# A 32-tile MLP at the end of a two-net kernel: 24 of its hidden tiles in pairs by Strassen's method, output rows between the products

## What is computed

```python
    u = rms_norm_2(h, norm_mlp_g[l])
    h = h + jnp.square(jax.nn.relu(u @ w_mlp1[l])) @ w_mlp2[l]
return rms_norm_2(h, final_norm_g)
```

## Time and profile before

| | |
|---|---|
| median of 3 runs | 2532.96 us (2532.82 to 2533.18) |
| the profiled execution | 2532.82 us |
| its span | 2531.0 us |
| TensorE (PE) busy | 2511.3 us, 99% |
| DVE busy | 1882.5 us, 74% |
| ACT busy | 1170.4 us, 46% |
| DMA queues, HBM | 97 GB/s over the span |

### The profile page before, as it was taken

The page is one execution under the profiler, slowest core; times in us unless marked ns, Lnnn a source line. Parts: engine busy times, 40 slices in busy tenths (PEclk is TensorE's granted clock), DMA queues, the critical chain, the costliest instruction groups (busy, mean ns, idle before and its releaser), DMA issues.

```text
span 2531.0 us, 35169 instructions
## 1 busy us (share of the span) xinstructions
PE 2511.3 (99%) x13914; PEld 2187.0 (86%) x13914; DVE 1882.5 (74%) x2579; ACT 1170.4 (46%) x1843; POOL 302.8 (12%) x250
## 2 busy tenths in 40 slices
PE   8999999999999999999999999999999999999999
PEld 7899988888999889999888899997888888788887
DVE  8878867777888687887786778876999786642433
ACT  5444445444444444444553444445587445432332
POOL 4000001320000000000024000000286231100001
PEclk9999999999999999999999999999999999999999
DMA  5333333233333323333423233334322423233332
GB/s 155 98 97 102 94 103 92 77 101 90 92 100 109 115 84 97 98 106 103 109 59 100 85 106 94 105 107 128 80 74 74 130 88 113 80 106 100 92 100 83
DMA packets 489962, 248.32 MB, mean 98 GB/s; under 512 B 41922, under 2 KB 486599, under 8 KB 489543
## 3 DMA queue, kind: packets, MB, share of 16 engines
q1 hardware_dynamic: 489346, 245.76, 33.5%
q10 hardware_dynamic: 452, 0.32, 0.1%
HBM read 241.84 MB, written 4.19 MB: 97 GB/s over the span
## 4 chain that ended last, share of the span: by engine, by line
PE 92%; DVE 5%; ACT 2%; issue 1%; DMA 0%; POOL 0%; DVEq 0%; ACTq 0%
PE bank L725 7%; PE bank L727 7%; PE bank L726 7%; PE bank L806 7%; PE bank L805 7%; PE bank L804 7%; PE psS L826 5%; PE psS L827 5%; PE psS L828 5%; PE psT L725 4%; PE psT L727 4%; PE psT L726 4%; PE psT L870 2%; PE psT L872 2%; PE psT L871 2%; PE psS L725 1%
## 5 line engine op out<-in xcount | busy, mean ns | idle before, releaser
L2004 DVE TENSOR_TENSOR wlo<-raw,whi 128x1024 fp32r<-128x1024 f32 (+1 forms) x274 | 362.8, 1326 | 116.7 <-ACT whi L1421 113.5
L725 PE MATMUL bank<-xhi,whi 128*128 128x512 f32 x888 | 349.4, 393 | 1.4 <-issue 1.4
L726 PE MATMUL bank<-xlo,whi 128*128 128x512 f32 x888 | 345.9, 390 | 0.0
L727 PE MATMUL bank<-xhi,wlo 128*128 128x512 f32 x888 | 345.8, 389 | 0.0
L1421 ACT ACTIVATE whi<-raw 128x1024 fp32r<-128x1024 f32 (+1 forms) x271 | 277.1, 1025 | 121.8 <-PE psT L727 92.4
L804 PE MATMUL bank<-xsh,whi 128*128 128x256 f32 x768 | 217.5, 283 | 0.9 <-ACT part L1534 0.7
L805 PE MATMUL bank<-xsl,whi 128*128 128x256 f32 x768 | 217.3, 283 | 0.0
L806 PE MATMUL bank<-xsh,wlo 128*128 128x256 f32 x768 | 217.3, 283 | 0.0
L2067 DVE TENSOR_TENSOR wlo<-tw,whi 128x1024 fp32r<-128x1024 f32 x128 | 156.9, 1226 | 63.1 <-ACT whi L1453 63.0
L826 PE MATMUL psS<-hhi,whi 128*128 128x512 f32 x512 | 200.8, 392 | 0.0
L827 PE MATMUL psS<-hlo,whi 128*128 128x512 f32 x512 | 200.8, 392 | 0.0
(11 more groups left out here) (586 smaller groups left out, 6444.4 us busy)
## 6 DMA issues: line engine op xcount, KB each, us to landing
raw<-in_ffn_wg SPq DMA_DIRECT2D x88, 512.0 KB
raw<-in_ffn_wu SPq DMA_DIRECT2D x88, 512.0 KB
raw<-in_w_mlp SPq DMA_DIRECT2D x64, 512.0 KB
raw<-in_w_in SPq DMA_DIRECT2D x53, 512.0 KB
raw<-in_ffn_wd SPq DMA_DIRECT2D x48, 256.0 KB
raw<-in_ffn_wd SPq DMA_DIRECT2D x32, 384.0 KB
raw<-in_ffn_wd SPq DMA_DIRECT2D x48, 192.0 KB
raw<-in_ffn_wd SPq DMA_DIRECT2D x48, 128.0 KB
```

The costliest lines, as they stand in the source:

```text
L725: pe.matmul(dest, a, rhs_hi(k), start=start and k == 0, stop=False)
L726: pe.matmul(dest, a, rhs_lo(k), start=False, stop=False)
L727: mm = pe.matmul(dest, b_, rhs_hi(k), start=False, stop=stop and k == tiles - 1)
L2004: dve.tensor_tensor(wlo[:, a:a + n], raw[:, a:a + n], whi[:, a:a + n].bitcast(F32), ALU.subtract).then_inc(s_split, 1)
```

## The change

The MLP is written like the windows. Tiles 0 to 7 are made as before (`MPLAIN`). Tiles 8 to 31 are made in 12 windows, two tiles each (`mlp_window`). The two passes are gone: the hidden tiles are in groups of 6, 6, 6, 6 and 8. The output rows of the first four groups (4 x 8 chunks x 6 tiles = 192 tiles of work) are cut in 25 units of 7 or 8, one ahead of the windows and two in each window, and each finished chunk of a group is added to x by DVE (`ffn_group_added`, `k_xa`). The last group's 8 chunks of 8 tiles follow the windows. The quarter sums of x are made beside tiles 2, 3, 4 and 5, each of which takes one unit of TensorE. Hidden tiles go into 14 places: 12 of `hhi`/`hlo` and two laid over buffers that are free by then. Three loads behind the end that no one read are gone.

```diff
+    MPLAIN, MHT = 8, HT + 2
+    MGROUPS = [(0, 6), (6, 12), (12, 18), (18, 24), (24, 2 * FP)]
+    MFAST = (2 * FP - MPLAIN) // 2
+    mlp_rows = [(grp, m, k) for grp, (f0, f1) in enumerate(MGROUPS[:-1]) for m in range(KC) for k in range(f1 - f0)]
+    MUNITS = [mlp_rows[len(mlp_rows) * i // (2 * MFAST + 1):len(mlp_rows) * (i + 1) // (2 * MFAST + 1)]
+              for i in range(2 * MFAST + 1)]
+    MSIDES = {(w, i): MUNITS[2 * w + 1 + i] for w in range(-1, MFAST) for i in range(2) if w >= 0 or i}
...
+        def hidden(tile):
+            s = tile % MHT
+            if s < HT:
+                return chunk(hhi, s), chunk(hlo, s)
+            return ((hid12h[:, :], hid12l[:, :]), (hid13h[:, :], hid13l[:, :]))[s - HT]
+
+        mlp_tiles = lambda grp: MGROUPS[grp][1] - MGROUPS[grp][0]
+        MLP_QUARTERS_AT = {2: 0, 3: 1, 4: 2, 5: 3}
...
-            for ps in range(2):
-                c0 = C_MLP + ps * U_PASS
-
-                def four(c, q, f, first):
-                    for j in range(4):
-
-
-                        if first and ps == 0 and j < 2:
-                            unit_by_terms(c + j, q, mlp_b[j], FINAL1 + 2, j == 0, between=mlp_sum)
-                        else:
-                            unit(c + j, q, mlp_b[j], KC, *xk())
-                four(c0, 0, ps * FP, True)
-                for it in range(1, FP // 4):
-                    four(c0, it * 4, it * 4 + ps * FP, False)
-                for mi in range(0, KC // 2):
-                    for m in range(2):
-                        pe.wait_ge(s_x, mi * 2 + ((FINAL1 + 3 + ps) * KC + m - 1))
-                        for j in range(2):
-                            if m == 0:
-                                pe.wait_ge(m_lo, ps * FP + 8 * j + 8)
-                            unit(c0 + FP + 2 * m + j, mi * 4, down_b[m], 8,
-                                 lambda k, j=j: chunk(mhi, 8 * j + k), lambda k, j=j: chunk(mlo, 8 * j + k),
-                                 start=j == 0, stop=j == 1)
...
+            def mlp_side(w, i):
+                for j, (grp, m, k) in enumerate(MSIDES[w, i]):
+                    r = grp * KC + m
+                    if k == 0 and r >= 3:
+                        pe.wait_ge(k_xa, FIRST_ADD + r - 2)
+                    elif k == 0 and r == 2:
+                        pe.wait_ge(m_r, MPLAIN)
+                    if m == 0:
+                        pe.wait_ge(m_lo, MGROUPS[grp][0] + k + 1)
+                    a, dest = (2 * i + 1) * UNIT + j * P, side_b[r % 3]
+                    hh, hl = hidden(MGROUPS[grp][0] + k)
+                    pe.matmul(dest, whi[:, a:a + P], hh, start=k == 0, stop=False)
+                    pe.matmul(dest, whi[:, a:a + P], hl, start=False, stop=False)
+                    mm = pe.matmul(dest, wlo[:, a:a + P], hh, start=False, stop=k == mlp_tiles(grp) - 1)
+                return mm
+
+            def mlp_window(w):
+                c, g = C_MLP + WINDOWS_AT + 4 * w, FIRST_G + w
+                bank_a, bank_c, bank_d = bank[0][:, 0:QT], bank[1][:, 0:QT], psT[:, 0:QT]
+                pe.wait_ge(k_lo, 4 * g + 1)
+                if w:
+                    pe.wait_ge(k_ev, 4 * g - 1)
+                else:
+                    pe.wait_ge(m_r, 5)
+                mlp_terms(bank_a, cwh, cwl, 0, mlp_corner(0, 0), True, True).then_inc(k_pe, 1)
+                if w:
+                    pe.wait_ge(k_ev, 4 * g - 3)
+                mlp_terms(bank_d, cwh, cwl, S, mlp_corner(4, 0), True, True).then_inc(k_pe, 1)
+                pe.wait_ge(k_lo, 4 * g + 2)
+                pe.wait_ge(k_sn, 3 * g + 1)
+                if w == 0:
+                    pe.wait_ge(k_xl, 8 * L + 4)
+                mlp_terms(bank_a, whi, wlo, 0, mlp_summed(1), False, True, True).then_inc(k_pe, 1)
+                if w:
+                    pe.wait_ge(k_ev, 4 * g)
+                else:
+                    pe.wait_ge(m_r, 6)
+                mlp_terms(bank_c, whi, wlo, S, mlp_summed(0), True, True).then_inc(s_used, 1)
+                pe.wait_ge(k_lo, 4 * g + 4)
+                pe.wait_ge(k_sn, 3 * g + 2)
+                mlp_terms(bank_a, whi, wlo, 2 * UNIT, mlp_summed(2), False, True, True).then_inc(k_pe, 1)
+                pe.wait_ge(k_lo, 4 * g + 3)
+                mlp_side(w, 0).then_inc(s_used, 1)
+                pe.wait_ge(k_sn, 3 * g + 3)
+                mlp_terms(bank_a, whi, wlo, 2 * UNIT + S, mlp_corner(4, QT), False, True, True).then_inc(s_used, 1)
+                pe.wait_ge(s_split, c + 3 + RING)
+                pe.wait_ge(k_ev, 4 * g + 2)
+                mlp_terms(bank_c, dwh, dwl, 0, mlp_summed(3), False, True, True).then_inc(k_pe, 1)
+                pe.wait_ge(s_split, c + 4 + RING)
+                mlp_side(w, 1).then_inc(s_used, 1)
...
+            for f in range(MPLAIN):
+                if f < 2:
+                    unit_by_terms(C_MLP + f, 0, mlp_b[f], FINAL1 + 2, f == 0, between=mlp_sum)
+                else:
+                    if f >= 4:
+                        pe.wait_ge(m_r, f - 3)
+                    unit(C_MLP + f, 0, mlp_b[f % 4], KC, *xk())
+            pe.wait_ge(s_split, C_MLP + MPLAIN + 1 + RING)
+            mlp_side(-1, 1).then_inc(s_used, 1)
+            for w in range(MFAST):
+                mlp_window(w)
+            n = mlp_tiles(-1)
+            pe.wait_ge(k_ev, 4 * (FIRST_G + MFAST) - 3)
+            pe.wait_ge(k_xa, FIRST_ADD + (len(MGROUPS) - 1) * KC - 1)
+            for k0, k1 in ((0, n - 1), (n - 1, n)):
+                pe.wait_ge(m_lo, MGROUPS[-1][0] + k1)
+                for m in range(2):
+                    pe.wait_ge(s_split, C_MLP + MLAST_AT + m + 1 + RING)
+                    mlp_last(m, k0, k1)
+            for m in range(2, KC):
+                pe.wait_ge(s_x, (FINAL1 + 3) * KC + m - 1)
+                pe.wait_ge(s_split, C_MLP + MLAST_AT + m + 1 + RING)
+                mlp_last(m, 0, n)
...
+            def mlp_window(w):
+                g, f = FIRST_G + w, MPLAIN + 2 * w
+                on = w + 1 < MFAST
+                if w:
+                    mlp_whole_hi(w, 1)
+                act.wait_ge(k_pe, 5 * g + 1)
+                act.wait_ge(k_ev, 4 * g - 3)
+                act.activation(part[0][:, :], bank[0][:, 0:QT], ACT.Copy).then_inc(k_sn, 1)
+                if w == 0:
+                    mlp_whole_hi(0, 1)
+                if on:
+                    mlp_corner_hi(w + 1)
+                act.wait_ge(k_pe, 5 * g + 3)
+                act.wait_ge(k_ev, 4 * g)
+                act.activation(part[2][:, :], bank[0][:, 0:QT], ACT.Copy).then_inc(k_sn, 1)
+                act.wait_ge(k_pe, 5 * g + 4)
+                act.wait_ge(k_ev, 4 * g - 2)
+                act.activation(part[1][:, :], bank[0][:, 0:QT], ACT.Copy).then_inc(k_sn, 1)
+                if on:
+                    mlp_sums_hi(w + 1, 0)
+                    mlp_whole_hi(w + 1, 0)
+                    mlp_sums_hi(w + 1, 1)
+                else:
+                    for j in range(AHEAD):
+                        mlp_ahead(MLAST_AT + j)
+                mlp_square(f, tmp[1], tmp[1])
+                if on:
+                    mlp_last_hi(w + 1)
+                mlp_square(f + 1, tmp[3], tmp[3])
+
+            for f in range(MPLAIN):
+                mlp_ahead(f + AHEAD)
+                if f == 0:
+                    root(MLPN)
+                if f in MLP_QUARTERS_AT:
+                    mlp_gained(MLP_QUARTERS_AT[f])
+                mlp_square(f, tmp[f % 2], tmp[2 + f % 2])
+                if f in MLP_QUARTERS_AT:
+                    mlp_quarters_hi(MLP_QUARTERS_AT[f])
+            mlp_ahead(MPLAIN + AHEAD)
...
+            def mlp_ahead(u):
+                if u == MPLAIN:
+                    split(C_MLP + u, 0, len(MSIDES[-1, 1]))
+                elif u == WINDOWS_AT:
+                    mlp_corner_lo(0)
+                    mlp_weight_sums(0)
+                    mlp_sums_lo(0, 0)
+                elif u == WINDOWS_AT + 1:
+                    mlp_whole_lo(0, 0)
+                elif u == WINDOWS_AT + 2:
+                    mlp_sums_lo(0, 1)
+                    mlp_last_lo(0)
...
+            def mlp_quarter_sums(i):
+                n = 16 * (2 * L) + 4 * i
+                near, far = xg2[:, 0:S], xg2[:, S:2 * S]
+                s1, s2, s3, s4 = (xsum[:, j * QT:(j + 1) * QT] for j in range(4))
+                dve.wait_ge(k_xg, 4 * (2 * L) + i + 1)
+                dve.wait_ge(k_xl, 4 * (2 * L) + i)
+                dve.tensor_tensor(s1, near[:, halves[1]], far[:, halves[1]], ALU.add).then_inc(k_xs, 1)
+                dve.tensor_tensor(s3, near[:, halves[0]], near[:, halves[1]], ALU.subtract).then_inc(k_xs, 1)
+                dve.wait_ge(k_xs, n + 1)
+                dve.tensor_tensor(s2, s1, near[:, halves[0]], ALU.subtract).then_inc(k_xs, 1)
+                dve.wait_ge(k_xs, n + 3)
+                dve.tensor_tensor(s4, far[:, halves[0]], s2, ALU.subtract).then_inc(k_xs, 1)
...
+            def mlp_side_adds(w, i):
+                ends = mlp_side_ends(w, i)
```

(101 more changed lines are left out.)

191 lines of the change are left out of this document (127 added, 64 removed).

## The result

The changed kernel takes 2536.6 us (median of 20; before, measured beside it, 2533.1): a ratio of 1.0014, 95% interval 1.0008 to 1.0021. That is 3.5 us more: clear of noise, but within the 0.2% set as no change. One of the 20 executions took 4084.3 us at a mean granted clock of 0.57 and is left out of the ratio. The profiled execution has a span of 2534.9 us, where before had 2531.0.

What follows compares the result with a forecast made beforehand. TensorE was taken to bound the last net, its time being number of matmuls times pitch. Against 2532.82 us, -9.1 + 7.5 + 1.5 + 0.95 + 0.1 = +0.95 gave 2533.8, range 2530 to 2537, chance 0.68.

Steps and rivals of the forecast that it cites:

- The saving on TensorE: Tiles 8 to 31: 84 narrow matmuls replace 48 wide ones per pair, saving 0.76 us a pair, 9.1 in all.
- the third chunk: At the end, the third output chunk waits for the first one's add, as in the first net: 0.1 us.
- The entry wait: First window: TensorE's third product waits for ACT's copy of `part0`, 7.5 us, bounded by 4.8 and 9.5.
- the quarter sums' period: Tiles 2 to 5: with the quarter sums DVE needs 5.53 us a tile, more than TensorE's 5.44.
- The clock: Behind the entry wait some 3 us run at 1.2 GHz, costing 1.5 us (0 to 1.7).
- The end wait: Last matmuls wait for DVE's add of the last but one output chunk: 0.95 us.
- No wait inside the windows: TensorE waits nowhere within the windows, each lasting 20.6 us.
- a window of more than 20.8 us: In the windows: a length listed among the signs that the prediction is wrong, against 20.6 us expected.
- the slower rival: Windows each wait for the second weight tile's late load: +11 us at 12 us of landing, 2545; chance 0.12.
- Close, but it holds: First window: DVE reaches the second quarter about 10.3 us after the wait; the seventh product needs it some 11.5 after.
- The first rival: Window entry: wait under 3 us and clock spared, 2526.8 us, or 2524.8 with no wait; chance 0.2.

Runs made afterwards that it cites:

- experiment 9: Changed kernel with experiment 6's entry order, experiment 7's weaker wait and small buffers moved so hidden tiles 12 and 13 lie like the others: 2525.1 us, ratio 0.9969.
- Experiment 2: Changed kernel with the quarter sums of x thinned to 8 to 32 columns in ACT's and DVE's operations: 2.4 us under the kernel before, ratio 0.9990.
- experiment 6: Experiment 5's kernel with DVE's second-quarter add in the first window moved right behind the low part of hidden tile 7: 5.8 us under the kernel before, 0.9977.
- Experiment 4: Changed kernel with 30 unread wide matmuls added on TensorE ahead of the first window's third product: 1.7 us over the kernel before, ratio 1.0007.
- experiment 7: Changed kernel whose last pass waits for one DVE add fewer: 2.5 us over the kernel before, ratio 1.0010.
- experiment 5: Changed kernel with the whole window entry re-ordered by need in ACT's and DVE's queues, nothing left out: 1.2 us under the kernel before, ratio 0.9996.

## Why the prediction was right, step by step

The forecast was 2533.8 us and the measured time is 2536.6, inside its own range of 2530 to 2537. The terms and their places came true; that a saving of 9.1 us is used up by one wait and what follows it was forecast. The sum came out short by 2.8 us, most of a difference of 3.5, since four terms were sized too small or left out.

- **The saving on TensorE, -9.1: right.** 84 narrow matmuls take 10.06 us and the passages between the shapes the rest. With every wait gone (experiment 9) the stage takes 296.2 us against 304.65, 8.4 less: the 9.1 without the 0.37 of the third chunk and the 0.3 of the second window.
- **The entry wait, 7.5: right in place, size and releaser.** It is 7.42 by the profile; `part0` was forecast to start at 2229.4 and starts at 2229.58, the quarter sums' period was 5.53 and is 5.55. The schedule held because each piece was a spacing from a row. The order of ACT's queue is part of it, but as a given. Not seen was that the order is what can be changed. "DVE's and ACT's list in this stretch is as long as it is: to hide it DVE would have to lose 7.5 of the 34 us" took the list's length for the cause. Experiment 2 shows that 5.2 us hang on the length, but experiment 6 removes all but 0.3 us of it at full length. Of the list, only what stands ahead of the copy counts.
- **The clock, +1.5 (0 to 1.7): right in kind, too small.** It cost 2.21 us, since half clock lasted 4.9 us behind the wait and not 3.4. Experiment 4 shows it apart: 2.14 us. This is the one term outside its own bounds; it was sized by the fall after the program's end, which says nothing of the rise. The prediction also reads 1.2 GHz off the slow transposes at the program's start; that rests on their durations alone, since the profile's granted clock is 1.00 in that stretch. The rule of the Trainium skill quoted in the prediction (TensorE: Matmul & The Clock Gate, "What's actually happening"), that idleness throttles and activity releases, agrees with the 0.50 of this stretch.
- **The end wait, 0.95: right.** 0.99 in the trace, and gone in experiment 7. **The third chunk, 0.1: too small,** 0.37 with the slow restart behind it.
- **No wait inside the windows: right.** They last 21.00 us with 16 side tiles and 20.32 with 15, 20.6 on average as forecast. By its letter the sign of being wrong, "a window of more than 20.8 us", is met by the ones with 16, but no wait is in them. The second weight tile never holds TensorE up, so the slower rival doesn't come. In the first window the second quarter is in time (2239.45 against 2243.47) only since TensorE had been waiting; in experiment 5, without that wait, it is late by 3.2 us. "Close, but it holds" was true by the grace of the first wait.
- **Not in the sum at all: what the wide matmuls take besides,** +0.99 us, 0.8 of it the longer pitch, and some 0.9 us upstream and in the output. The errors are 0.7, 0.3, 1.0 and 0.9, all to one side: 2536.6 and not 2533.8.
- The first rival (a small entry wait) named 2524.8 for no wait at all; with the waits taken away by order and the pitch mended the kernel stands at 2525.1.

## What to carry to other kernels

When an engine waits for another that has time to spare, try the order of that engine's queue first: move the step that is waited for ahead of the work for later, and look where the wait turns up next. Here it turned up in three places (`part0`, `part2`, second quarter) before it was gone, and the order gave back 9.3 us with no work removed. A stage that is cheaper on the bounding engine pays only if its entry does; 9.1 us saved over 12 windows were lost in one place of 10 us. In these runs a gap of 2 to 7 us on TensorE cost 1.6 to 2.2 us beyond itself, so hiding all of it was worth more than its length.
